# Gated linear attention: outputs of two heads at a time, taking turns between the two halves of TensorE's rows

## What is computed

```
qe  = q * exp(b);   ke = k * exp(-b)          # b: decays summed up inside a chunk
att = einsum('bhnld,bhnmd->bhnlm', qe, ke) * lower
o   = einsum('bhnlm,bhnme->bhnle', att, v) + einsum('bhnld,bhnde->bhnle', qe, s_prev)
o   = rmsnorm(o_forward + o_backward) * silu(g)
```

## Time and profile before

| what | value |
|---|---|
| median of 3 runs | 3347.0 us (3345.62 to 3349.86) |
| the profiled execution, own time | 3339.85 us |
| its span, first to last instruction | 3338.2 us |
| TensorE matmul busy | 2806.9 us (84%) |
| VectorE busy | 1643.3 us (49%) |
| ScalarE busy | 941.1 us (28%) |
| GpSimd busy | 753.0 us (23%) |
| mean granted TensorE clock | 0.907 |

### The profile page before, as it was taken

One profiled execution on the slowest core, in us unless ns is written; L12 is line 12 of the kernel. 1 busy time (PEld: TensorE's weight loads), 2 busy tenths in 40 slices (PEclk: granted clock), 3 DMA queues, 4 the chain that ended last, 5 costly groups with the idle time before them and its releaser, 6 DMA issues. The chain is left out here.

```text
span 3338.2 us, 41678 instructions
## 1 busy us (share of the span) xinstructions
PE 2806.9 (84%) x14724; PEld 2062.9 (62%) x14724; DVE 1643.3 (49%) x3017; ACT 941.1 (28%) x1469; POOL 753.0 (23%) x353
## 2 busy tenths in 40 slices
PE   3996777994996875995886988999999787789997
PEld 2774355332775454332676677878888574578886
DVE  5896742334797643233651755373536306441113
ACT  3224422113223523212312733112122313232222
POOL 1440020110441020110230031232333210034443
PEclk9997986997997886997888998999999898899999
DMA  6530017963541015972451011241323220022322
GB/s 243 198 133 32 1 38 282 343 221 118 174 167 44 1 38 208 347 266 91 147 181 70 1 64 59 74 157 57 127 105 133 84 85 1 26 101 84 105 91 73
DMA packets 92340, 398.17 MB, mean 119 GB/s; under 512 B 16384, under 2 KB 17952, under 8 KB 70816
## 3 DMA queue, kind: packets, MB, share of 16 engines
q1 hardware_dynamic: 63248, 303.42, 25.4%
q0 software_dynamic: 28800, 92.30, 7.7%
q10 hardware_dynamic: 144, 0.52, 0.0%
HBM read 490.04 MB, written 23.59 MB: 154 GB/s over the span
## 5 line engine op out<-in xcount | busy, mean ns | idle before, releaser
L2340 DVE TENSOR_TENSOR ffn_silu<-ffn_silu,PS 128x512 f32<-128x512 f32 x66 | 37.5, 596 | 418.9 <-ACT ffn_silu L2322 418.9
L375 POOL TENSOR_TENSOR 21_w_part<-weights_raw,21_w_part 128x2048 fp32r<-128x2048 f32 (+2 forms) x44 | 147.5, 3354 | 404.7 <-ACT 21_w_part L337 404.7
L2082 PE MATMUL PS<-one_weights_more,12_h_tokens 128*64 128x512 f32 (+1 forms) x1024 | 231.1, 604 | 2.5 <-ACT 12_h_tokens L2134 1.7
L223 PE MATMUL PS<-ffn_h_parts,21_w_part 128*128 128x512 f32 (+1 forms) x640 | 203.5, 338 | 8.6 <-DVE ffn_out_t L1576 7.8
L224 PE MATMUL PS<-ffn_h_parts,21_w_part 128*128 128x512 f32 (+1 forms) x640 | 202.4, 338 | 0.0
L375 POOL TENSOR_TENSOR 35_w_part<-weights_raw,35_w_part 128x2048 fp32r<-128x2048 f32 (+2 forms) x36 | 149.1, 4144 | 213.3 <-ACT 35_w_part L337 213.3
L375 POOL TENSOR_TENSOR 3_w_part<-weights_raw,3_w_part 128x1024 fp32r<-128x1024 f32 (+1 forms) x52 | 143.1, 2754 | 140.3 <-ACT 3_w_part L337 139.8
L2082 PEld LDWEIGHTS PS<-one_weights_more,12_h_tokens 128*64 128x64 f32 x1024 | 78.4, 139 | 133.1 <-issue 129.3
L2322 ACT ACTIVATE ffn_silu<-PS 128x512 f32<-128x512 f32 x66 | 32.4, 526 | 404.1 <-PE PS L228 378.4
L223 PE MATMUL PS<-one_mix_h_parts,3_w_part 128*128 128x512 f32 x352 | 143.9, 409 | 0.2
L224 PE MATMUL PS<-one_mix_h_parts,3_w_part 128*128 128x512 f32 x352 | 137.9, 392 | 0.0
(11 more groups left out here) (626 smaller groups left out, 6925.2 us busy)
## 6 DMA issues: line engine op xcount, KB each, us to landing
one_weights_more<-in_w_gu SPq DMA_DIRECT2D x128, 1024.0 KB, 9.8
one_weights_more<-in_w_down SPq DMA_DIRECT2D x64, 1024.0 KB, 8.7
weights_raw<-in_f_gu SPq DMA_DIRECT2D x44, 1024.0 KB, 4.8
one_values<-in_w_ada POOLq DMA_DIRECT2D x32, 1024.0 KB, 5.2
weights_raw<-in_w_proj SPq DMA_DIRECT2D x60, 512.0 KB, 3.3
ffn_shared<-in_w_ada POOLq DMA_DIRECT2D x24, 1024.0 KB, 6.7
weights_raw<-in_w_ada SPq DMA_DIRECT2D x32, 512.0 KB
two_ab_mod_w<-in_w_ada POOLq DMA_DIRECT2D x16, 1024.0 KB, 5.3
```

The lines of the kernel that those rows point to most:

```text
L223: nc.tensor.matmul(out, w[0], x[1], start=(j == 0), stop=False)
L375: self.nc.gpsimd.tensor_tensor(self.part[:, u, 1], self.raw[:, u], self.part[:, u, 0].bitcast(F32), ALU.subtract).then_inc(self.count["spl ...
L2082: mm = nc.tensor.matmul(M.PS[rows(h), 2 + i % 2, :], h_[:, i % 2, k, rows(h)], weights(i, h, k * 2 * FE), start=(k == 0), stop=(k == KD - 1))
L2340: ins = nc.vector.tensor_tensor(sl[:, u, off:off + nt], sl[:, u, off:off + nt], M.PS[:, 4 * u + 2 + a, 0:nt], ALU.mult)
```

## The change

The loop goes over p = 0 .. 7 instead of n = 0 .. 15: a pair of heads (2c, 2c + 1) and a token tile. e = 0 and 1 is the head within the pair, and `rows(e)` its 64 rows.

- `scores(p)`: four matmuls, in the order direction, then head: rows 0 to 63, rows 64 to 127, rows 0 to 63, rows 64 to 127. Head 0 of the pair writes bank 6*(p % 2), head 1 bank 6*(p % 2) + 1, so banks 0, 1, 6 and 7 hold scores. `att` is raised once for the pair.
- The mask on VectorE stays at 16 instructions of the same size, two for each pair. `am` has four slots in place of two.
- `values(p)`: four matmuls of 128 rows (head 0 twice, head 1 twice), then eight of 64 rows, in which the head changes with every instruction. It waits for both masks of the pair. `pv` is raised once for the pair.
- Ahead of the matmuls with ones, which write banks 6 and 7, TensorE waits for all 16 masks.
- ScalarE's square of head h waits for all four tiles of the pair that h belongs to.

```diff
-            def scores(n):
-                h, t = n // TT, n % TT
-                b, c = 64 * (h % 2), h // 2
-                if n >= 2:
-                    pe.wait_ge(s["masked"], n - 1)
+            def scores(p):
+                c, t = p // TT, p % TT
+                if p >= 2:
+                    pe.wait_ge(s["masked"], 2 * (p - 1))
                 for d in range(2):
-                    mm = nc.tensor.matmul(M.PS[:, n % 2, d * P:(d + 1) * P], B.ke[b:b + 64, 2 * d + c, t * P:(t + 1) * P],
-                                          B.qe[b:b + 64, 2 * d + c, t * P:(t + 1) * P], start=True, stop=True)
+                    for e in range(2):
+                        mm = nc.tensor.matmul(score_bank(p, e)[:, d * P:(d + 1) * P],
+                                              B.ke[rows(e), 2 * d + c, t * P:(t + 1) * P],
+                                              B.qe[rows(e), 2 * d + c, t * P:(t + 1) * P], start=True, stop=True)
                 mm.then_inc(s["att"], 1)
...
+            def values(p):
+                c, t = p // TT, p % TT
+                pe.wait_ge(s["masked"], 2 * p + 2)
+                for e in range(2):
+                    for d in range(2):
+                        nc.tensor.matmul(result(p, e), B.V[:, t, (2 * c + e) * P:(2 * c + e + 1) * P],
+                                         am[:, 2 * (p % 2) + e, d * P:(d + 1) * P], start=(d == 0), stop=False)
                 for d in range(2):
                     for j in range(2):
-                        at = t * P + j * 64
-                        last = d == 1 and j == 1
-                        mm = nc.tensor.matmul(M.PS[:, 2 + h, at:at + 64], B.Sp[b:b + 64, d, c, 2 * t + j, :],
-                                              B.qe[b:b + 64, 2 * d + c, at:at + 64], start=False, stop=last)
+                        for e in range(2):
+                            at = t * P + j * 64
+                            last = d == 1 and j == 1
+                            mm = nc.tensor.matmul(result(p, e)[:, j * 64:(j + 1) * 64], B.Sp[rows(e), d, c, 2 * t + j, :],
+                                                  B.qe[rows(e), 2 * d + c, at:at + 64], start=False, stop=last)
                 mm.then_inc(s["pv"], 1)
...
+            pe.wait_ge(s["masked"], 2 * N)
             for h in range(4):
                 pe.wait_ge(s["sq"], h + 1)
...
             for h in range(4):
-                act.wait_ge(s["pv"], TT * (h + 1))
+                act.wait_ge(s["pv"], TT * (h // 2 + 1))
                 nc.scalar.activation(sq[:, h, :], M.PS[:, 2 + h, :], ACT.Square).then_inc(s["sq"], 1)
```

More of the change, by code:

```diff
@@ L2956, in gla_outputs @@
     with ExitStack() as ctx:
-        am = ctx.enter_context(M.nc.sbuf_tensor(f"{M.blocks}_gla_att", [P, 2, 2 * P], F32))
+        am = ctx.enter_context(M.nc.sbuf_tensor(f"{M.blocks}_gla_att", [P, 4, 2 * P], F32))
         hw = ctx.enter_context(M.nc.sbuf_tensor(f"{M.blocks}_gla_hw", [P, 2], F32))
@@ L2961, in gla_outputs, with score_bank, result, rows @@
         block = ctx.enter_context(nc.Block())
-        N = 4 * TT
+        N = 2 * TT
+        def score_bank(p, e):
+            return M.PS[:, 6 * (p % 2) + e, 0:2 * P]
+        def result(p, e):
+            return M.PS[:, 2 + 2 * (p // TT) + e, p % TT * P:(p % TT + 1) * P]
+        def rows(e):
+            return slice(64 * e, 64 * e + 64)
         @block.sync
@@ L2993, in values @@
                 mm.then_inc(s["pv"], 1)
             keep_clock(nc, M, M.PS[:, 7, :], 4)
[L2996 to L3000, removed]
+            for p in range(N + 1):
+                if p < N:
+                    scores(p)
+                if p >= 1:
+                    values(p - 1)
+            pe.wait_ge(s["masked"], 2 * N)
             for h in range(4):
@@ L3009, in _ @@
         def _(dve):
[L3010 to L3014, removed]
+            for n in range(2 * N):
+                p, e = n // 2, n % 2
+                dve.wait_ge(s["att"], p + 1)
+                if p >= 2:
+                    dve.wait_ge(s["pv"], p - 1)
+                nc.vector.tensor_tensor(am[:, 2 * (p % 2) + e, :], score_bank(p, e), B.K2[:, J_MASK:J_MASK + 2 * P],
                                         ALU.mult).then_inc(s["masked"], 1)
```

## The result

The changed kernel takes 3337.34 us, the median of 20 runs. The kernel before, run again beside it, has a median of 3351.53 us over 20 runs; the ratio of the two is 0.9947 with a 95% interval of 0.9929 to 0.9965. That is 14 us between the medians and 17.8 us (11.7 to 23.8) by the ratio. The time lies within 1 us of the forecast of 3336.6; the gain is larger than the 10.4 us that I worked out, and 10.4 (a ratio of 0.9969) lies outside of the interval. Both facts need a reason, and they have two different ones.

What follows compares the result with a forecast made beforehand. TensorE was taken to bound the block's first stretch, VectorE its tail. The stretch falls from 32.75 to 21.7 us, less 0.62 on ScalarE: 10.4 off the 3347.0 median gives 3336.6 us, range 3331.5 to 3342.

Steps and rivals of the forecast that it cites:

- start, first scores to first values: Start of the block's stretch: first values need two masks, 0.45 us more than 1.23, so 1.68 us.
- step of a pair: TensorE's scores, values and states for two heads take 2.62 us, where two steps before took 4.36 or 3.56.
- saved in the stretch: First scores to last states on TensorE: 32.75 us before, 21.7 after, so 11.05 us saved.
- second square behind it: ScalarE behind the stretch: two squares instead of one stand there, adding 0.62 us that nothing hides.
- States in turns: A pair's sixteen state records alternate between row halves in eight slots, 0.95 us if all overlap, 1.83 if none do.
- rival 2: States of a pair overlap in part (chance 0.07, 3340.1 us) or not at all (chance 0.05, 3343.6 us).
- Rival 1: No matmul record starts ahead of one written before it: 1.8 us less gained, 3338.4 us; chance 0.05.
- Rival 3: Nothing overlaps in scores or states: a step takes 3.94 us, 3346.7 us in all, no change; chance 0.05.
- rival 4: TensorE's array empties at each change of half, 80 in all: 16 us more, 3362.7 us, slower; chance 0.04.
- Nothing behind the block takes the gain up: After the block TensorE is busy 358.58 of 376.20 us, so what the stretch saves, the program saves.
- the paragraph on the clock: TensorE's clock stays at 1.00 in the stretch; its return behind the tail leaves 1.8 us of uncertainty.
- 1.8 us for such things: Uncertainty in one execution from when TensorE's full clock returns behind the tail, half of 3.63 us either way.

Runs made afterwards that it cites:

- one head after the other: Changed kernel with all of one head's scores, and likewise states, before the other's inside a pair: 3340.47 us, ratio 0.994 to the kernel before.
- experiment on one half: Changed kernel with the second head's scores and states computed from the first head's rows (wrong output, timing only): 3355.77 us, ratio 0.9974.
- new tail: Changed kernel with one root and one reciprocal serving all four heads, spread again by four 32-row matmuls: 3327.86 us, ratio 0.9895.
- repeated: The changed kernel run again with nothing edited: 3337.87 us, ratio 0.9931 to the kernel before.
- by steps: Kernel before with its sixteen steps reordered, heads 0, 0, 1, 1 and so on, so scores follow the other half's states: 3343.22 us, ratio 0.9952.
- filled: Kernel before with one more 128-row, 256-column matmul in each step, into a bank nobody reads: 3353.27 us, ratio 0.9987.

## Why the prediction was right, and where it was not

**The sum of the block.** Each of its terms can be read off the profile after:

| term | predicted us | measured us |
|---|---|---|
| start, first scores to first values | 1.68 | 1.58 |
| step of a pair | 2.62 | 2.63 |
| scores, values, states of a step | 0.59, 1.08, 0.95 | 0.60, 1.09, 0.94 |
| saved in the stretch | 11.05 | 11.04 |
| second square behind it | 0.62 | 0.5 |
| saved, first scores to block end | 10.4 | 10.6 |

The start is shorter because masks on end follow each other after 0.34 us (four in 1.42 us), not 0.45. The table's last line is the saving that the forecast rests on, and it holds.

**States in turns,** the form that the trace before did not hold, go at two per slot throughout (sixteen records in 1.11 us). The step rested on the few records in the earlier trace rows, and that was enough: rival 2 is out. Rival 1, strict order, is out twice: in the changed kernel no slot is lost, and with one head after the other TensorE passes the written order by three records. Rival 3 described the experiment on one half to 0.02 us a step; in the changed kernel it is out, as is rival 4: a change of half costs nothing.

**Nothing behind the block takes the gain up.** This was argued from TensorE's share there. The profiles show it: from the block's end to the program's end it is 441.7 to 444.3 us in all eleven, whichever kernel ran and whether the block took 40.6 us (the new tail) or 77.5. The new tail agrees, 8.6 us less in the block and 10.0 less in the time.

**The step that failed** is the paragraph on the clock: "The stretch is at 1.00 and stays so, with TensorE no less busy." For the changed kernel's stretch it is right in all three profiles that have it (first, repeated, new tail: 1.00 throughout), but not for the reason given: the kernel on one half has TensorE busy all the time and loses the clock. For the kernel before it took one profiled execution and three runs for all of its executions. Of the 71 undisturbed runs of it that I have with a clock, 42 lie in the group of 0.900 and below; the one of them that was profiled lost the clock inside this very stretch, at a price of 16 us. That the other 41 did so too is concluded from their times and mean clocks. None of the changed kernel's 30 undisturbed runs is of that kind, and this is the part of the gain that the forecast does not have. A loss late in its short stretch would cost only a few us and not show in a mean clock, so for runs that were not profiled it is not excluded; their times spread over 14 us, those of the shorter kind of the kernel before over 13. Against the shorter kind of run the gain is near what was predicted, 3346.8 - 3337.3 = 9.5 us (median of the 11 runs below 3353 us in the first comparison), and 3345.4 - 3337.9 = 7.5 us in the second (ten runs), a difference that the scatter of single runs allows; against the longer kind, a median of 3366.8 us in the first, it is 29 us. The median before that I started from, 3347.0, was that of three runs of the first kind, so the predicted time came out right and the predicted difference too small. That was luck: nine of the other 17 runs in that comparison are of the longer kind, and three of those would have put the forecast some 20 us too high.

**A term of scatter.** The four matmuls on constants ahead of the scores took 5.0 us in the profile before and 6.7 in the first one after. In eleven profiles it is 5.0 to 6.7 with either kernel: they begin at half clock, and it comes back at another moment. I had 1.8 us for such things, looked for behind the block, where the first profile after lost 1.2; this one is 1.6 more, ahead of it.

## What to carry to other kernels

Work that fills half of TensorE's rows is worth putting in turns with the other half's, instruction by instruction and into different banks: two 64-row records then cost what one did here, and going by blocks gives only what lies within about three records of the change. Look at such a change twice, once for the slots and once for the clock: a kernel whose runs fall into two groups by mean granted clock may be losing it in a stretch that looks perfectly busy, and a profile of the better kind will not show it. When a block ends in one engine's chain over equal parts, look for the operation that costs the same for all parts together; here that was worth as much as the change itself.

## What the runs showed of the hardware

- TensorE can lose its clock with hardly a pause. With 64-row matmuls on one half at a time beside 128-row ones it fell to 0.50 after 13.1 us (kernel before) and after 18.3 us (one half alone), with matmuls busy 13.03 of 13.10 and 18.30 of 18.30 us. With the halves overlapping, even for only part of each step, or with a full matmul more per step, none of 64 undisturbed runs (30 changed, 10 head after head, 12 by steps, 12 filled) is of the longer kind, their mean clocks are all 0.902 or more, and the five profiles among them have 1.00 for the whole stretch. Both kernels that lost it work on one half for most of a step; whether it is the share of rows at work, the kind of matmul or something else that decides was not tried. The Trainium skill, "TensorE: Matmul & The Clock Gate" (Why this matters for your kernels), asks for an engine kept busy without idle gaps; these stretches had gaps of 0.07 us in all or none, and that was not enough.
- Loads of 128 columns of weights for the two halves go side by side: state records, 0.11 us apart on one half, come in pairs at the same 0.11 us, and sixteen matmul records last 1.11 us in place of eight in 1.10.
- A record of the other half starts ahead of up to three that are written before it (and the kernel with head after head), but matmuls over all rows wait for both halves (0.20 us from the last start to the next, with or without overlap).
- Which kind of run the kernel before falls into differs from launch to launch on one chip (18 of 28 runs on one, then 18 of 28 and 5 of 12 on another are of the longer kind). What decides it stays open.
